# A 31-tap depthwise convolution dealt out anew between ScalarE, GpSimd and VectorE, and a mixing layer in another order

## The chip, the cores and the metric

One Trainium2 chip, one of its cores. The number is the device time of one execution in microseconds; smaller is better. The kernel is a single launch that computes two transformer-like blocks in fp32 for 512 positions of width 1024.

## The reference, cut to what matters

The change lies in the mixing layer of the first block. Everything is fp32; `u` is 512 x 1024.

```python
u = modulate(x, sh2, sc2)
proj = u @ w_in                                    # 1024 x 6144
xr, gr, conf_in, gate_a, gate_b = split(proj)      # 1024, 1024, 2048, 1024, 1024 columns

xr = causal_depthwise_conv(xr, rnn_conv_w, rnn_conv_b)     # 4 taps
r, i = sigmoid(xr @ w_r + b_r), sigmoid(xr @ w_i + b_i)    # per head, 8 heads of 128
log_a = -8 * softplus(-lam) * r
h = scan(exp(log_a), sqrt(-expm1(2 * log_a)) * (i * xr))   # linear recurrence over positions
ya = (h * gelu(gr)) @ rnn_w_proj

glu = conf_in[..., :1024] * sigmoid(conf_in[..., 1024:])
hb = causal_depthwise_conv(glu, conf_dw_w, conf_dw_b)      # 31 taps
hb = silu(layer_norm(hb, conf_ln_g, conf_ln_b))
yb = hb @ conf_w_proj

merged = sigmoid(gate_a) * ya + sigmoid(gate_b) * yb
x = layer_norm(ALPHA * x + (1 + g2) * (merged @ mix_w_out), ln2_g, ln2_b)
```

## The kernel before

Activations lie with features on the partitions: a tensor of 512 x 1024 is eight tiles f = 0..7 of 128 x 512. A product with a weight matrix is made in chunks. A chunk is 256 output columns: its 1 MB of weights comes by DMA from SyncE's queue into one of two slots of `WRAW`; ScalarE copies it rounded to fp32r into `WHI` (`hi`, L555), VectorE makes the rest `WLO` (`lo`, L975), and TensorE runs 48 matmuls of 128x128 by 128x512 (two tiles, eight k, three products of high and low parts; `gemm_chunk`, L1758). ScalarE may overwrite a slot when the chunk two before is done, TensorE starts a chunk when `WLO` is made (`w_lo`) and when its pair of PSUM banks was read out (`free0` or `free1`). `PHASES` (L60) gives the order of all chunks; `CB` and `UB` are the numbers at which a phase begins. Every engine works through its own list in the written order; a wait holds all that is behind it on that engine.

The phases of the mixing layer, in the order of TensorE before the change: `conf` (8 chunks, the input of the long convolution), `xr` (4), `gr` (4), then 16 single matmuls `ri` for r and i (L1960 to L1967), `gb` (4), `ga` (4), `ya` (4), `yb` (4), `mix` (4).

- ScalarE: after each `hi` it reads out PSUM. `conf`: sigmoid into `STG` (L684). `xr`: copy into `XR`. `gr`: gelu into `G` (L697), which lies in the 16 KB of scratch per partition at `T0`. `ri`: sigmoid, tanh, exp (L703 to L712). `gate` (L714): sigmoid of `gb` and `ga` into `STG`, then a store to DRAM; `STG` shares its place with `IT`, the scratch of the recurrence, so a gate first waits until VectorE's 16 steps with it are done (`bt_step` 16). Later it loads the gates back (`SGA`, `SGB`).
- The 31 taps of a tile are 31 multiply-adds over 512 positions. VectorE does tiles 3 to 7 (`conv_taps`, L1232), one instruction a tap, with the running sum in PSUM bank 7; it inserts a written number of taps after its `lo` steps. GpSimd does tiles 0 to 2 (L452 to L466), two instructions a tap: a TENSOR_SCALAR into `TAP`, and a TENSOR_TENSOR that adds it to `HB`.
- VectorE besides: the 4-tap convolution (L1270, L1273), products of the recurrence (L1282 to L1293), then for each tile the scan and the product with gelu (`scan`, L1300), the split of `h * gelu` into `YH` and `YL`.
- The layer norm of the convolution: GpSimd sums six tiles (`ln_sum`, L420), TensorE makes a shift of it (`ln_shift(1)`, ahead of `ya`), VectorE subtracts it, ScalarE squares, GpSimd sums the squares, TensorE makes the statistics (`ln_stats(1)`, after `ya`), VectorE normalizes, ScalarE applies silu, and both split the result into `YH` and `YL` for `yb`.

Of the kernel before, what the change touches and what calls it, by code (L numbers as in the profile page):

```python
# [38 lines left out]
POOL_CONV = 3  # L39
# [20 lines left out]
PHASES = [("ffn1", 22, 11), ("down1", 16, 4), ("conf", 8, 4), ("xr", 4, 2), ("gr", 4, 2),  # L60
          ("gb", 4, 2), ("ga", 4, 2), ("ya", 4, 2), ("yb", 4, 2), ("mix", 4, 2),
# [35 lines left out]
def build_program(nc, I, out):  # L97
    ctx = ExitStack()
    with ctx:
        BASE = 16512  # L100

        def at(name, kb, shape, dt=F32):
# [20 lines left out]
        TAP = at("conv_tap", H0 + 85, [P, L])  # L123
# [5 lines left out]
        STG = at("stage4k", H0 + 81, [P, 2, L])  # L129
# [19 lines left out]
        CONF_T = (at("conf_x_sum", 80, [P, L]), at("conf_squares_sum", 82, [P, L]), at("conf_squares", 84, [P, 2, L]))  # L149
        ln_tiles = lambda c: CONF_T if c == 1 else LN_T  # L150

# [108 lines left out]
                 "yb_sum mg_hi mg_lo lam_step conv31 conv31p s5_load s5_pow_load s5_expand s5_t "  # L260
# [21 lines left out]
        def _(sp):  # L282
# [113 lines left out]
        def _(pool):  # L396
# [54 lines left out]

            for f in range(POOL_CONV):  # L452
                pool.wait_ge(s["free1"], UB["conf"] + f // 2 + 1)
                if f == 0:
                    pool.wait_ge(s["pads_ready"], 1)
                for k in range(CONV_C):
                    src = GLU[:, f, k + 2:k + 2 + L]
                    w = col("conf_dw_w_a", 8 * k + f)
                    n = (2 * CONV_C - 1) * f + 2 * k
                    if k == 0:  # L460
                        nc.gpsimd.tensor_scalar(HB[:, f], src, w, col("conf_dw_b", f), ALU.mult, ALU.add).then_inc(s["conv31p"], 1)
                        continue
# [89 lines left out]
        def _(act):  # L552
# [127 lines left out]
            with act.Fori(0, 4) as i:  # L680
# [6 lines left out]
            act.wait_ge(s["pads_ready"], 2)  # L687
            with act.Fori(0, 2) as i:
                for j in range(2):
                    hi_step("xr", i, 2, j)  # L690
                    act.wait_ge(s["mm"], CB["xr"] + 2 * i + j + 1)
                    A(XR[:, bass.ds(4 * i + 2 * j, 2), 8:8 + L], PS[:, 2 * j:2 * j + 2], ACT.Copy).then_inc(free[j], 1)
            with act.Fori(0, 2) as i:
                for j in range(2):
                    hi_step("gr", i, 2, j)
                    act.wait_ge(s["mm"], CB["gr"] + 2 * i + j + 1)
                    A(G[:, bass.ds(4 * i + 2 * j, 2)], PS[:, 2 * j:2 * j + 2], ACT.Gelu_apprx_tanh).then_inc(free[j], 1)  # L697

            for f in range(KT):
# [13 lines left out]

            def gate(ph, dram, i, j):  # L714
                hi_step(ph, i, 2, j)
                n = (4 if ph == "ga" else 0) + 2 * i + j
                act.wait_ge(s["mm"], CB[ph] + 2 * i + j + 1)
                act.wait_ge(s["bt_step"], 16)
                if n:
                    act.wait_ge(s["sgb_store"], 16 * n)  # L720
                A(STG[:], PS[:, 2 * j:2 * j + 2], ACT.Sigmoid).then_inc(free[j], 1)
                act.wait_ge(free[j], UB[ph] + i + 1)
                act.dma_start(dram[:, 4 * i + 2 * j:4 * i + 2 * j + 2, :], STG[:]).then_inc(s["sgb_store"], 16)
            gate("gb", sgb_dram, 0, 0)
            gate("gb", sgb_dram, 0, 1)
# [29 lines left out]
            act.wait_ge(s["xn_ready"], 16)
# [216 lines left out]
        def _(dve):  # L972
# [38 lines left out]
            def ln_normalize(c, src, each, rooting=None):  # L1011
# [13 lines left out]
                dve.wait_ge(s["ln_step"], ln_step(V.reciprocal(RSTD[:], RT[:])))  # L1025

                def scaled(f):
# [3 lines left out]
                    V.tensor_tensor(src[:, f], src[:, f], RSTD[:], ALU.mult).then_inc(s["xn_ready"], 1)  # L1031
# [197 lines left out]
            taps = [(f, k) for f in range(POOL_CONV, KT) for k in range(CONV_C)]  # L1229
# [19 lines left out]
            for i in range(4):  # L1249
# [5 lines left out]
                if i >= 2:  # L1255
                    conv_taps((16, 15)[i - 2])
# [18 lines left out]
            for i in range(2):  # L1275
                for j in range(2):
                    lo_step("gr", i, 2, j)
                    conv_taps((8, 8, 8, 7)[2 * i + j])
# [4 lines left out]
            lo_step("gb", 0, 2, 0)  # L1283
# [11 lines left out]
            lo_step("gb", 0, 2, 1)  # L1295
# [918 lines left out]
```

## Time and profile before

| | us |
|---|---|
| median of 3 runs | 2374.69 |
| the 3 runs | 2377.97, 2372.64, 2374.69 |
| the profiled execution, its own time | 2371.09 |
| its span (first to last instruction) | 2369.1 |
| TensorE busy in the span | 1953.8 (82%) |
| VectorE | 1205.8 (51%) |
| ScalarE | 743.1 (31%) |
| GpSimd | 488.9 (21%) |

The page cuts the span into 40 slices of 59 us; a digit is the busy share of an engine in tenths. TensorE's row is 3999999799978085979999998869996677496877: slices 13 and 15 (0 and 5 where the neighbours have 8 and 9) lie from 770 to 948 us, in the mixing layer. Matmuls overlap in the pipeline, so a busy share is read for where it falls, not for its height.

### The profile page before, as it was taken

The numbers are of one execution on the slowest core, as the hardware profiler recorded it, in microseconds if no ns is written. First come the engines' busy times: TensorE is split into PE (matmuls) and PEld (weight loads), VectorE is DVE, ScalarE is ACT, GpSimd is POOL, SyncE is SP. The second block draws the span as 40 slices with busy tenths as digits, with TensorE's granted clock in tenths as the row PEclk, the third lists the DMA queues.
The fourth block names the chain that finished last, engine by engine and source line by source line (L and its number), as shares of the span: only waits on it lengthen the run. The fifth ranks groups of instructions, "written<-read, shape, count | busy, mean of one in ns | idle before, by whom it ended". The sixth has DMA issues, their size and how long they took to land.

```text
span 2369.1 us, 23466 instructions
## 1 busy us (share of the span) xinstructions
PE 1953.8 (82%) x8848; PEld 1566.9 (66%) x8848; DVE 1205.8 (51%) x1463; ACT 743.1 (31%) x723; POOL 488.9 (21%) x386
## 2 busy tenths in 40 slices
PE   3999999799978085979999998869996677496877
PEld 2788878588757064758888877768873357474645
DVE  4555555639958476463323346633286764144223
ACT  2433322442453013244333335412341211122323
POOL 0311111279999910010000020010000030100000
PEclk8999999899989597989999999979997785698989
DMA  7455554223313211213333234452321070422200
GB/s 254 154 183 178 175 160 148 84 89 107 107 54 124 71 53 67 90 39 107 95 100 97 87 104 134 145 107 81 107 87 64 9 118 29 107 89 89 71 1 36
DMA packets 201885, 236.71 MB, mean 100 GB/s; under 512 B 5627, under 2 KB 184603, under 8 KB 200923
## 3 DMA queue, kind: packets, MB, share of 16 engines
q1 hardware_dynamic: 185067, 171.27, 22.9%
q0 software_dynamic: 14736, 54.04, 8.7%
q10 hardware_dynamic: 2016, 10.49, 1.2%
q8 instruction: 44, 0.72, 0.1%
q14 instruction: 22, 0.18, 0.0%
HBM read 220.58 MB, written 15.20 MB: 100 GB/s over the span
## 4 chain that ended last, share of the span: by engine, by line
PE 36%; DVE 8%; issue 4%; ACT 4%; DMA 4%; POOL 1%; DVEq 0%; ACTq 0%; SPq 0%; POOLq 0%
PE ps L1769 12%; PE ps L1937 9%; PE ps L1821 4%; PE ps L1787 2%; DMA w_raw<-in_s_glu_w 1%; PE ps L2121 1%; PE ps L2127 1%; DVE ret_root L1629 1%; ACT w_hi L559 1%; PE ps L2143 1%; PE ps L1877 1%; PE ps L2045 1%; DMA s_in<-u_scratch 1%; PE ps L2166 1%; DVE w_lo L978 1%
## 5 line engine op out<-in xcount | busy, mean ns | idle before, releaser
L978 DVE TENSOR_TENSOR w_lo<-w_raw,w_hi 128x2048 fp32r<-128x2048 f32 x160 | 375.3, 2345 | 774.3 <-ACT w_hi L559 757.5
L559 ACT ACTIVATE w_hi<-w_raw 128x2048 fp32r<-128x2048 f32 x158 | 302.4, 1914 | 977.5 <-PE ps L1769 547.6
L1769 PE MATMUL ps<-u_hi,w_hi 128*128 128x512 f32 x960 | 383.7, 400 | 72.7 <-DVE u_lo L1692 31.3
L1769 PE MATMUL ps<-u_lo,w_hi 128*128 128x512 f32 x960 | 378.5, 394 | 0.0
L1769 PE MATMUL ps<-u_hi,w_lo 128*128 128x512 f32 x960 | 378.2, 394 | 0.0
L1769 PEld LDWEIGHTS ps<-u_hi,w_hi 128*128 128x128 f32 x960 | 184.0, 192 | 117.8 <-issue 54.8
L1937 PE MATMUL ps<-u_hi,w_hi 128*128 128x512 f32 x656 | 256.9, 392 | 0.3 <-ACT silu_gate L637 0.3
L1937 PE MATMUL ps<-u_lo,w_hi 128*128 128x512 f32 x656 | 255.8, 390 | 0.0
L1937 PE MATMUL ps<-u_hi,w_lo 128*128 128x512 f32 x656 | 255.8, 390 | 0.0
L1769 PEld LDWEIGHTS ps<-u_lo,w_hi 128*128 128x128 f32 x960 | 183.7, 191 | 39.1 <-issue 1.3
L1769 PEld LDWEIGHTS ps<-u_hi,w_lo 128*128 128x128 f32 x960 | 183.1, 191 | 39.0
L464 POOL TENSOR_SCALAR conv_tap<-glu,param_cols 128x512 f32<-128x512 f32 x90 | 187.6, 2085 | 8.8
L1821 PE MATMUL ps<-hid_hi,w_hi 128*128 128x512 f32 x352 | 140.6, 400 | 0.6 <-DVE hid_lo L1148 0.6
L1937 PEld LDWEIGHTS ps<-u_hi,w_hi 128*128 128x128 f32 x656 | 123.5, 188 | 26.0 <-ACT silu_gate L637 0.7
L1937 PEld LDWEIGHTS ps<-u_hi,w_lo 128*128 128x128 f32 x656 | 123.6, 188 | 25.8
L1937 PEld LDWEIGHTS ps<-u_lo,w_hi 128*128 128x128 f32 x656 | 123.6, 188 | 25.4
L1821 PE MATMUL ps<-hid_hi,w_lo 128*128 128x512 f32 x352 | 137.7, 391 | 0.0
L1821 PE MATMUL ps<-hid_lo,w_hi 128*128 128x512 f32 x352 | 137.6, 391 | 0.0
L466 POOL TENSOR_TENSOR conv_out<-conv_out,conv_tap 128x512 f32<-128x512 f32 x90 | 126.9, 1409 | 7.5
L1244 DVE SCALAR_TENSOR_TENSOR ps<-glu,param_cols,ps 128x512 f32<-128x512 f32 x145 | 109.5, 755 | 4.7
L408 POOL DMA_DIRECT2D ada_raw<-in_ada_w x56 | 40.1, 717 | 347.2 <-DVE ada_acc L1082 295.7
L1082 DVE SCALAR_TENSOR_TENSOR ada_acc<-ada_raw,silu_c,ada_acc 128x512 f32<-128x512 f32 x98 | 74.2, 757 | 8.1 <-DMA ada_raw<-in_ada_w 5.5
(423 smaller groups left out, 2800.2 us busy)
## 6 DMA issues: line engine op xcount, KB each, us to landing
w_raw<-in_w_in SPq DMA_DIRECT2D x44, 1024.0 KB, 5.2
ada_raw<-in_ada_w POOLq DMA_DIRECT2D x56, 512.0 KB, 5.0
w_raw<-in_ffn_w_gate SPq DMA_DIRECT2D x22, 1024.0 KB, 5.3
w_raw<-in_ffn_w_up SPq DMA_DIRECT2D x22, 1024.0 KB, 5.3
w_raw<-in_ffn_w_down SPq DMA_DIRECT2D x32, 704.0 KB, 4.6
ada_first<-in_ada_w SPq DMA_DIRECT2D x8, 1024.0 KB, 11.3
w_raw<-in_w_out SPq DMA_DIRECT2D x8, 1024.0 KB, 5.0
w_raw<-in_rnn_w_proj SPq DMA_DIRECT2D x4, 1024.0 KB, 5.6
```

What stands on the lines that cost most here:

```text
L408: pool.dma_start(ADRAW[:, q % 2], wk8(I["ada_w"])[:, 2 * q:2 * q + 2, bass.ds(2 * D + 512 * i, 512)]).then_inc(ada_load[q % 2], 16)
L464: nc.gpsimd.tensor_scalar(TAP[:], src, w, None, ALU.mult).then_inc(s["conv31p"], 1)
L466: nc.gpsimd.tensor_tensor(HB[:, f], HB[:, f], TAP[:], ALU.add).then_inc(s["conv31p"], 1)
L559: A(WHI[:, slot], WRAW[:, slot], ACT.Copy).then_inc(s["w_hi"], 1)
L978: V.tensor_tensor(WLO[:, slot], WRAW[:, slot], WHI[:, slot].bitcast(F32), ALU.subtract).then_inc(s["w_lo"], 1)
L1082: ins = V.scalar_tensor_tensor(out=acc, in0=ADRAW[:, q % 2, kk], scalar=SC[:, k:k + 1], in1=acc, op0=ALU.mult, op1=ALU.add)
L1244: ins = V.scalar_tensor_tensor(out=dst, in0=src, scalar=w, in1=HACC, op0=ALU.mult, op1=ALU.add)
L1629: V.reciprocal(RRT[:], RRT[:]).then_inc(s["rn"], 1)
L1769: ins = M(PS[:, 2 * j + t, 0:n], w[:, j, at_:at_ + P], a[:, k, 0:n], start=(q == 0), stop=(q == 3 * KT - 1))
L1787: ins = M(PS[:, 2 * j + t], w[:, j, at_:at_ + P], a[:, k], start=(k == 0 and q == 0), stop=(k == KT - 1 and q == 2))
L1821: ins = M(PS[:, 2 * (j // 2)], w[:, j % 2, P * kk:P * kk + P], a[:, k], start=(k == 0 and q == 0), stop=(k == FT - 1 and q == 2))
L1937: ins = M(PS[:, 2 * j + t], w[:, j, at_:at_ + P], a[:, k], start=(q == 0), stop=(q == 3 * KT - 1))
```

## The change

`POOL_CONV` is now tiles 0, 2, 4, 6 and `DVE_CONV` tiles 1, 3, 5, 7. For the first four ScalarE makes the product of each tap (Copy with a scale, or Identity with scale and bias for the first, straight into `HB`) into a ring of four tiles `TAP`, in portions of six after its own steps, and GpSimd only adds. The order of the phases becomes `conf`, `xr`, `gb`, `ri`, `ga`, `gr`, `ya`, `yb`; SyncE's stream follows. `STG` has a place of its own, `G` holds one pair of tiles instead of eight, and `SGA`, `SGB` and the split of the norm's result (`CHI`, `CLO`) lie elsewhere. On TensorE the norm's shift and statistics stand between the chunks of `ya`. ScalarE's loops over `conf`, `xr` and `gr` are written out.

```diff
+POOL_CONV = (0, 2, 4, 6)
+DVE_CONV = (1, 3, 5, 7)
 # PHASES: ... conf, xr, gb, ga, gr, ya ...

 # GpSimd
+            for i, f in enumerate(POOL_CONV):
+                for k in range(1, CONV_C):
+                    m = (CONV_C - 1) * i + k - 1
+                    pool.wait_ge(s["conv_tap"], CONV_C * i + k + 1)
+                    if m:
+                        pool.wait_ge(s["conv31p"], m)
+                    nc.gpsimd.tensor_tensor(HB[:, f], HB[:, f], TAP[:, m % 4], ALU.add).then_inc(s["conv31p"], 1)

 # ScalarE
+            def conv_products(n):
+                for f, k in products[made[0]:made[0] + n]:
...
+                        m = (CONV_C - 1) * i + k - 1
+                        if m >= 4:
+                            act.wait_ge(s["conv31p"], m - 3)
+                        ins = A(TAP[:, m % 4], src, ACT.Copy, scale=w)
...
+            for i in range(4):
                 hi_step("conf", i, 2, 0)
...
                 A(STG[:], PS[:, 0:2], ACT.Sigmoid).then_inc(s["free0"], 1)
+                if i:
+                    conv_products(6)
                 hi_step("conf", i, 2, 1)
+                if i:
+                    conv_products(6)
 # xr, gb: hi_step, PSUM read out (gb also stored), conv_products(6), four times each; then ri as before
-                act.wait_ge(s["bt_step"], 16)
+            gate("ga", sga_dram, 0)
             for f in range(KT):
                 act.wait_ge(s["bt_step"], 2 * f + 2)
                 A(TB[:, f], TB[:, f], ACT.Sqrt).then_inc(s["rnn_sqrt"], 1)
+            for n in range(1, 4):
+                gate("ga", sga_dram, n)
+                conv_products(6)
+            for n in range(4):
+                act.wait_ge(s["mm"], CB["gr"] + n + 1)
+                if n:
+                    act.wait_ge(s["yf_ready"], n)
+                A(G[:], PS[:, 2 * (n % 2):2 * (n % 2) + 2], ACT.Gelu_apprx_tanh).then_inc(free[n % 2], 1)
+                hi_step("gr", n // 2, 2, n % 2)
+                conv_products(6)
+                act.wait_ge(s["yf_ready"], n + 1)
+                A(YH[:, 2 * n:2 * n + 2], XC[:, 2 * n:2 * n + 2], ACT.Copy).then_inc(s["yh_ready"], 2)
             act.wait_ge(s["sgb_store"], 128)
+            act.wait_ge(s["mm"], CB["ya"])
             act.dma_start(SGA[:], sga_dram).then_inc(s["sg_load"], 16)
             hi_step("ya", 0, 2, 0)
             hi_step("ya", 0, 2, 1)
+            ln_squares(1, HB, 0, 8)
             hi_step("ya", 1, 2, 0)
             ln_root(1)
             for f in range(KT + 1):
...
+                if f == 3:
+                    hi_step("ya", 1, 2, 1)

 # VectorE: conv_taps(18) in conf i = 1..3 (before: 16, 15 in i = 2, 3); 8 after each gb step;
 # none after the products of the recurrence; all eight scans behind the two steps of ga i = 0; 6 after each step of ga i = 1
+            for n in range(4):
+                dve.wait_ge(s["scan_done"], 2 * KT)
+                dve.wait_ge(free[n % 2], UB["gr"] + n // 2 + 1)
+                xp = XC[:, 2 * n:2 * n + 2]
+                V.tensor_tensor(xp, xp, G[:], ALU.mult).then_inc(s["yf_ready"], 1)
+                lo_step("gr", n // 2, 2, n % 2)
+                conv_taps(3)
+                dve.wait_ge(s["yh_ready"], 2 * n + 2)
+                V.tensor_tensor(YL[:, 2 * n:2 * n + 2], xp, YH[:, 2 * n:2 * n + 2].bitcast(F32), ALU.subtract).then_inc(s["yl_ready"], 2)
             dve.wait_ge(s["sg_load"], 16)
+            conv_taps(14)
+            lo_step("ya", 0, 2, 0)
+            ya_pair(0)
+            lo_step("ya", 0, 2, 1)
+            ya_pair(1)
+            ln_shift(1, HB, 0, 8)
+            lo_step("ya", 1, 2, 0)
+            ya_pair(2)
+            # ln_normalize; behind its tile 3: ya_pair(3), lo_step("ya", 1, 2, 1)

 # TensorE
             gemm("xr", 2, UH, UL)
+            gemm("gb", 2, UH, UL)
...
             gemm("ga", 2, UH, UL)
+            gemm("gr", 2, UH, UL)
+            gemm_chunk("ya", 0, 0, YH, YL, ready=lambda k: (s["yl_ready"], k + 1))
+            gemm_chunk("ya", 0, 1, YH, YL)
             ln_shift(1)
+            gemm_chunk("ya", 1, 0, YH, YL)
             ln_stats(1, HB, 7)
+            gemm_chunk("ya", 1, 1, YH, YL)
+            gemm_after("yb", 2, CHI, CLO, lambda k: (s["yl_ready"], 8 + k + 1))
```

`lo_step(ph, i, 2, j)` makes the weights of the chunk two further on: that of `gr` with n = 3 makes those of `ya`'s second chunk, that of `ya` (1, 1) those of `yb`'s second.

## Rows read from the trace of the kernel before

**Rows 1.** Who TensorE waited for, 600 to 1010 us: total, times, longest.

```profile
PE ps L1851 <- POOL conf_x_sum L430: 64.9, 1, 64.9
PE ps L1864 <- DVE conv_out L1009: 17.5, 1, 17.5
PE ps L1769 <- ACT stage4k L721: 13.8, 1, 13.8
PE ps L1787 <- DVE y_lo L1337: 10.8, 2, 10.4
...
PE ps L1769 <- DVE ya L1327: 4.1, 1, 4.1
PE ps L1769 <- DVE stage4k L1348: 3.0, 1, 3.0
```

**Rows 2.** Busy time by stretch: PE, PEld, DVE, ACT, POOL, then clock, DMA share, GB/s.

```profile
563.60:639.80 76.20, 76.20 (x338) 63.04 (x337) 75.31 (x68) 25.19 (x18) 72.75 (x40) 1.00 0.31 100
639.80:968.70 328.90, 210.85 (x811) 159.74 (x811) 215.66 (x222) 96.58 (x111) 189.49 (x114) 0.81 0.23 77
```

**Rows 3.** Timeline of ScalarE, weight copies released by a chunk's end: start, duration, idle before.

```profile
639.83 1.91 ACT L559 ACTIVATE w_hi<-w_raw 128x2048 fp32r<-128x2048 f32 x1 [6.62 <-PE ps L1769]
...
708.35 1.92 ACT L559 ACTIVATE w_hi<-w_raw 128x2048 fp32r<-128x2048 f32 x1 [4.06 <-PE ps L1769]
...
968.68 1.92 ACT L559 ACTIVATE w_hi<-w_raw 128x2048 fp32r<-128x2048 f32 x1 [3.04 <-PE ps L1769]
```

**Rows 4.** Timeline of TensorE: last matmul of `ri`; first of the third `gb` chunk.

```profile
657.88 1.12 PE L1967 MATMUL ps<-xr_conv,rglru_w 128*128 128x512 f32 x2
...
694.58 0.79 PE L1769 MATMUL ps<-u_hi,w_hi 128*128 128x512 f32 x1 [13.77 <-ACT stage4k L721]
```

**Rows 5.** The page's costliest groups: GpSimd's two instructions of a tap.

```profile
L464 POOL TENSOR_SCALAR conv_tap<-glu,param_cols 128x512 f32<-128x512 f32 x90 | 187.6, 2085 | 8.8
L466 POOL TENSOR_TENSOR conv_out<-conv_out,conv_tap 128x512 f32<-128x512 f32 x90 | 126.9, 1409 | 7.5
```

**Rows 6.** Timeline of GpSimd: four sums in a row, VectorE idle.

```profile
823.83 5.48 POOL L430 TENSOR_TENSOR conf_x_sum<-conf_x_sum,conv_out 128x512 f32<-128x512 f32 x4
```

**Rows 7.** Timeline of ScalarE: eight activations with a scale per partition.

```profile
660.20 5.01 ACT L709 ACTIVATE rnn_t<-rnn_a,lam_cols 128x512 f32<-128x512 f32 x8
```

**Rows 8.** Timeline of VectorE, 732 to 742 us: a weight rest, then the scans.

```profile
732.05 2.29 DVE L978 TENSOR_TENSOR w_lo<-w_raw,w_hi 128x2048 fp32r<-128x2048 f32 x1 [3.92 <-ACT w_hi L559]
734.26 1.78 DVE L1302 TENSOR_TENSOR rnn_t<-rnn_t,xr_conv 128x512 f32<-128x512 f32 x1
...
739.33 0.68 DVE L1302 TENSOR_TENSOR rnn_t<-rnn_t,xr_conv 128x512 f32<-128x512 f32 x1
740.05 1.51 DVE L1305 TENSOR_TENSOR_SCAN xr_conv<-rnn_a,rnn_t 128x512 f32<-128x512 f32 x1
```

**Rows 9.** Timeline of GpSimd: the addition that falls into these.

```profile
732.50 3.00 POOL L466 TENSOR_TENSOR conv_out<-conv_out,conv_tap 128x512 f32<-128x512 f32 x1
```

**Rows 10.** Timeline of VectorE: one step of the 4-tap convolution and the next weight rest.

```profile
571.03 1.79 DVE L1270 TENSOR_SCALAR xr_conv<-xr_pad,param_cols  x2
572.74 7.00 DVE L1273 SCALAR_TENSOR_TENSOR xr_conv<-xr_pad,param_cols,xr_conv  x6
579.67 3.38 DVE L978 TENSOR_TENSOR w_lo<-w_raw,w_hi 128x2048 fp32r<-128x2048 f32 x1
```

**Rows 11.** The page's groups: VectorE's taps, and a multiply-add all in SBUF elsewhere.

```profile
L1244 DVE SCALAR_TENSOR_TENSOR ps<-glu,param_cols,ps 128x512 f32<-128x512 f32 x145 | 109.5, 755 | 4.7
...
L1082 DVE SCALAR_TENSOR_TENSOR ada_acc<-ada_raw,silu_c,ada_acc 128x512 f32<-128x512 f32 x98 | 74.2, 757 | 8.1 <-DMA ada_raw<-in_ada_w 5.5
```

**Rows 12.** Timeline of VectorE: the norm's first and last steps by tile.

```profile
913.03 1.29 DVE L1031 TENSOR_TENSOR conv_out<-conv_out,rstd 128x512 f32<-128x512 f32 x2
...
934.17 1.29 DVE L1337 TENSOR_TENSOR y_lo<-conv_out,y_hi 128x512 fp32r<-128x512 f32 x2 [1.40 <-ACT y_hi L753]
```

**Rows 13.** The DMA view, issues: the gate's load, KB each, us to landing.

```profile
sig_gate_a<-sga_scratch ACTq DMA_DIRECT2D x1, 2048.0 KB, 8.1
```

More of the change, by code:

```diff
@@ L678, in _ @@
             ln_modulate_hi(0, 0, 8, 0)
-            with act.Fori(0, 4) as i:
+            products = [(f, k) for f in POOL_CONV for k in range(CONV_C)]
+            made = [0]
+            def conv_products(n):
+                for f, k in products[made[0]:made[0] + n]:
+                    src = GLU[:, f, k + 2:k + 2 + L]
+                    w = col("conf_dw_w_a", 8 * k + f)
+                    i = POOL_CONV.index(f)
+                    if k == 0:
+                        act.wait_ge(s["free1"], UB["conf"] + f // 2 + 1)
+                        ins = A(HB[:, f], src, ACT.Identity, scale=w, bias=col("conf_dw_b", f))
+                    else:
+                        m = (CONV_C - 1) * i + k - 1
+                        if m >= 4:
+                            act.wait_ge(s["conv31p"], m - 3)
+                        ins = A(TAP[:, m % 4], src, ACT.Copy, scale=w)
+                    ins.then_inc(s["conv_tap"], 1)
+                    made[0] += 1
+            act.wait_ge(s["pads_ready"], 2)
+            for i in range(4):
                 hi_step("conf", i, 2, 0)
@@ L684, in _, with gate @@
                 A(STG[:], PS[:, 0:2], ACT.Sigmoid).then_inc(s["free0"], 1)
+                if i:
+                    conv_products(6)
                 hi_step("conf", i, 2, 1)
[L687 to L697, printed above, removed]
+                if i:
+                    conv_products(6)
+            for n in range(4):
+                hi_step("xr", n // 2, 2, n % 2)
+                act.wait_ge(s["mm"], CB["xr"] + n + 1)
+                A(XR[:, 2 * n:2 * n + 2, 8:8 + L], PS[:, 2 * (n % 2):2 * (n % 2) + 2], ACT.Copy).then_inc(free[n % 2], 1)
+                conv_products(6)
+            def gate(ph, dram, n):
+                hi_step(ph, n // 2, 2, n % 2)
+                m = (4 if ph == "ga" else 0) + n
+                j = n % 2
+                act.wait_ge(s["mm"], CB[ph] + n + 1)
+                if m:
+                    act.wait_ge(s["sgb_store"], 16 * m)
+                A(STG[:], PS[:, 2 * j:2 * j + 2], ACT.Sigmoid).then_inc(free[j], 1)
+                act.wait_ge(free[j], UB[ph] + n // 2 + 1)
+                act.dma_start(dram[:, 2 * n:2 * n + 2, :], STG[:]).then_inc(s["sgb_store"], 16)
+            for n in range(4):
+                gate("gb", sgb_dram, n)
+                conv_products(6)
             for f in range(KT):
@@ L1227, in _ @@
             ln_normalize(0, X, ln_modulate_lo(0, 0, 8))
-            taps = [(f, k) for f in range(POOL_CONV, KT) for k in range(CONV_C)]
+            taps = [(f, k) for f in DVE_CONV for k in range(CONV_C)]
             done = [0]
@@ L1274, in _ @@
                             ins.then_inc(s["conv4"], 1)
[L1275 to L1278, printed above, removed]
+            for n in range(4):
+                lo_step("gb", n // 2, 2, n % 2)
+                conv_taps(8)
             for f in range(KT):
```

146 lines of the change are left out of this document (51 added, 95 removed).

## The prediction

> **What bounds the kernel now.** I read the slices first: TensorE is busy nearly everywhere except in the mixing layer. There the waits of TensorE name the places [rows 1]. The longest, 64.9 us, is one wait of `ln_shift(1)`, which stands ahead of `ya`, for GpSimd's sum of the convolution; then 17.5 for VectorE's last taps ahead of the statistics, 13.8 for the gate's `STG`, 10.8 for the norm's result, 4.1 and 3.0 for readouts. By stretch [rows 2]: from 563.6 to 639.8 TensorE has no gap at clock 1.00, seven chunks in 76.2 us, 10.88 us a chunk. From 639.8 to 968.7, the ends of `gr` and of `yb` [rows 3], it has 16 chunks (174.1 us), the 16 matmuls of `ri` (to about 658.4, 18.6 us [rows 4]) and the norm's six matmuls, for which I set 5.6 us (an estimate from their busy time). 328.9 - 198.3 = 130.6 us are idle time or slow clock (0.81 on the mean). This is the sum from which the change can take.
>
> GpSimd needs two instructions a tap [rows 5]: 2085 + 1409 ns and the gaps, 3.6 us, times 93 taps, all of 334 us. It began as soon as it could. So before, GpSimd's list is the path from the middle of `conf` to `ya`.
>
> **What goes.** ScalarE makes 124 products and GpSimd 120 additions. A sum of this shape takes GpSimd 5.48 / 4 = 1.37 us, gaps included [rows 6]; 120 of them 164 us. A product costs ScalarE 5.01 / 8 = 0.63 us (an activation with a scale per partition, [rows 7]). A portion of six is thus 3.8 us of ScalarE and 8.2 us of GpSimd, in a chunk of 10.88. The ring of four lets ScalarE finish a portion about 6 us after its start; with the weight copy (1.92) and the PSUM readout (1.0) it is back in 9 us. Behind a portion there wait the next `hi`, and so `lo` and TensorE; 9 < 10.88 covers it, and a portion of 8 us would end the cover. The portions end with the last `gr` chunk (the last has four), so the additions end some 3 us later, the sum of six tiles (5 x 1.37 = 6.9) lies beside `ya`'s first two chunks (21.8), and the 64.9 us go. The 13.8 go with `STG`'s own place, and with them the slow restart (the chunk begun at 694.58 ended at 708.35: 13.8 instead of 10.9, +2.9 [rows 3, 4]). VectorE has 124 taps instead of 155: 31 x 0.79 (755 ns [rows 11] and a gap) = 24 us less, and only 14 are left for after `gr`.
>
> **What comes in its place**, in TensorE's order:
> 1. *VectorE's own work against the additions, `xr` and `gb`.* The taps with their sum in PSUM keep 755 ns whatever GpSimd does. Instructions with two SBUF inputs don't. A step of the 4-tap convolution took 1.79 + 7.00 = 8.65 us from start to next start [rows 10], against 8 x 0.757 = 6.06 by the free multiply-add [rows 11]: 2.6 us more, beside some 2.5 additions of GpSimd, so 1.05 us each. The same at 734.26: 1.78 against 0.68, while the addition begun at 732.50 ran 3.00 (it waited for `w_lo` to end) [rows 8, 9]. They take turns. After the change six additions fall into each step instead of 2.5: 6.06 + 6 x 1.05 + 2.29 for `w_lo` = 14.65 us, against a chunk of 10.88: 3.8 too long, four times 15, less 2 us that VectorE is ahead: 13 us. Lower end 0 (GpSimd waits each time, VectorE never: 8.35 < 10.88); upper end 23 (a full addition of 1.37 each: 16.6 a step). I take 13, what the nearest rows give. The `gb` steps (2.3 + 8 x 0.79 = 8.6) only stop the loss.
>    The Trainium skill, "SBUF — State Buffer", section "SBUF: two separate sides", says that VectorE with two SBUF inputs and GpSimd take turns on one port pair, each for the whole instruction. By that this item would be near its upper end, 23, and the forecast 10 us later. Rows 8 and 9 agree as to the addition; rows 10 don't for GpSimd's one-input product, which lies beside VectorE's work nearly free.
> 2. *`ri`.* ScalarE comes to it behind a portion, and VectorE behind 8 taps instead of 7: +2 us (0 to 4). `ga`'s first two chunks cover tanh, exp and the products; GpSimd is idle there, and the weight rest of the third `ga` chunk, now behind all 16 of VectorE's steps, is ready as it is needed: 0 (0 to 5).
> 3. *Scans.* Now 0.68 + 1.51 us each, without the product with gelu (2.2, [rows 8]), but the last four lie beside two portions: two additions each, 4 x (2.2 + 2 x 1.05) = 17 us and 2.3 for `w_lo`, where TensorE gives about 12.5: +6.8 us ahead of `gr` (0 to 10).
> 4. *`gr` to `ya`.* gelu, product, `YH`, `YL` of the last pair come behind the last `gr` chunk: gelu 1.0, weight copy 1.9, four products 3, `YH` 1.1, `YL` 1.2 and hand-overs, 9 us, of which `ya`'s first six k (18 matmuls, 4.1) hide half: 4.7, and 2.5 for the additions beside it: 7.2 (4 to 10).
> 5. *`ya`.* VectorE waits for the gate's load (8.1 us, [rows 13], now issued after `gr`), then makes 14 taps (11.0), then the rest of weights and the readout for the third chunk: 3.1 late (1 to 6). The statistics wait for GpSimd's sum of squares: 3.5 (2 to 7), instead of 17.5.
> 6. *`yb`.* The normalization takes about 7 us to its first tile and then 22.4 (913.03 to 935.4, [rows 12]), beside `ya`'s last chunk (10.9). But `yb` begins only when its second chunk's weights are made, behind tile 3 (half of the 22.4, 11.2) plus copy, readout and rest (5.4), 0.8 after the statistics in all 24.4 - 10.9 = 13.5: I set 13.4 us of idleness, and 2.9 of slow clock; before, 10.8 and its slow clock. Then 1.5 for a readout. 17.8 together (12 to 26).
>
> Sum: 13 + 2 + 6.8 + 7.2 + 3.1 + 3.5 + 17.8 = 53.4 us in the place of 130.6: 77 us less. What follows `yb` is unchanged. The profiled execution took 2371.1, so 2294; it lies 3.6 below the median of the runs: **2297 us**.
>
> Besides, the page "ScalarE: Activation LUTs" of the Trainium skill, section "What ACT_TABLE_LOAD costs", counts about 1.38 us of drain on top of each load; the loads here stand as 1283 ns, and by the page the one ahead of gelu and the two of the norm would add up to 4 us to the forecast.
>
> **The rivals.**
> - *The port costs nothing* (GpSimd waits, VectorE doesn't). For it: GpSimd's addition at 732.50 did wait; and its additions leave gaps of 2.7 us in a chunk. Against it: rows 10. Items 1, 3 and 2.5 of item 4 go, 22 us, less 2 for a later VectorE in `xr`: 2277.
> - *The ring holds ScalarE.* If the additions come at 2.0 us, as in turns of 0.7 and 1.3, a portion of six needs 12 us > 10.88: 1.1 x 20 portions = 22, and item 1 at its upper end, 10 more: 2329. For it: its mean of 1409 ns and a gap [rows 5] are already over the free 1.37 [rows 6]. Against: VectorE works with two SBUF inputs in only part of the time.
> - *The norm's tail is longer.* Everything up to `ya` as forecast, but the interleaving of copies behind tile 3 and a restart at low clock cost 15 more: 2312.
> - *Slower.* One mechanism: ScalarE is in order, and a product may wait for an addition four back. If the additions take 3.0 us as that of 732.50 throughout, 3.1 with the gap, a portion takes 18.6, each chunk from the second pair of `conf` to `gr` ends 7.7 late, 20 x 7.7 = 154 us, against the 97 that the change brings without items 1 and 3: 2374.7 + 57 = 2432. It decides from a pitch p with 20 x (6p - 10.88) = 97, p = 2.6 us. Against it: in 90 additions the mean was 1.4.
>
> **How the numbers follow.** Forecast 2297: 0.47; port free 2277: 0.26; ring 2329: 0.14; tail 2312: 0.09; slower 2432: 0.04. The range goes from 2268 (port free, and items 4 to 6 at their lower ends) to 2328; it holds the first two, the tail and about half of the ring case. Less than 0.2%, 5 us, can't be told from no change: faster 0.95, same 0.01, slower 0.04, the last rival's chance and a remainder.
>
> **What would show it.** The wait of `ln_shift(1)` gone (under 2 us), the wait on `STG` gone; 120 additions with a mean of 1.5 to 1.9 us; the 4-tap step at 12 to 13 us and waits of TensorE for `w_lo` of 10 to 20 us in `xr`, `gb` and at `gr`'s start, near none if the port is free; ScalarE's weight copies released by the chunk's end and not by GpSimd (the ring rival turns that round); an idle stretch of 10 to 17 us ahead of `yb`. The forecast is wrong if TensorE still waits over 10 us for GpSimd, or if the stretch from the start of `conf` to the end of `yb` is not shorter by 60 to 95 us.

## The result, and the profile after

| | before | after |
|---|---|---|
| median of the runs, us | 2374.03 (4 runs) | 2303.65 (4 runs, 2299.68 to 2307.67) |
| ratio | | 0.9701, 95% interval 0.9679 to 0.9723 |
| profiled execution, us | 2371.1 | 2305.54, span 2303.9 |
| mean granted clock | 0.901 | 0.912 |

The kernel is 70.4 us faster; 77 were forecast, and the time lies in the predicted range.

First the page of the changed kernel, its costliest groups: line, engine, operation, names, count | busy, mean ns | idle before them and who ended it. They answer to [rows 5, 7, 11].

```profile
L463 POOL TENSOR_TENSOR conv_out<-conv_out,conv_tap 128x512 f32<-128x512 f32 x120 | 199.2, 1660 | 141.3 <-ACT conv_tap L693 126.0
...
L693 ACT ACTIVATE conv_tap<-glu,param_cols 128x512 f32<-128x512 f32 x120 | 79.6, 715 | 33.0 <-POOL conv_out L463 30.4
L1268 DVE SCALAR_TENSOR_TENSOR ps<-glu,param_cols,ps 128x512 f32<-128x512 f32 x116 | 87.6, 755 | 6.1 <-DMA sig_gate_a<-sga_scratch 2.4
```

GpSimd's convolution is 199 us of work instead of 315 (187.6 + 126.9 in [rows 5]), and it now has spare time: it waits 126 us for products. An addition takes 1660 ns on the mean, more than the 1409 of [rows 5]. VectorE's taps with the sum in PSUM still take 755 ns.

The waits of TensorE, 480 to 960 us (total, times, longest), answer to [rows 1].

```profile
PE ps L1801 <- DVE w_lo L1001: 16.9, 7, 7.2
PE ps L1819 <- DVE w_lo L1001: 12.8, 1, 12.8
PE ps L1801 <- DVE y_lo L1341: 8.1, 2, 7.5
PE ps L1999 <- ACT rnn_a L733: 5.7, 1, 5.7
PE ps L1801 <- DVE u_lo L1385: 5.1, 1, 5.1
PE ps L1896 <- POOL conf_squares_sum L447: 4.9, 1, 4.9
...
PE ps L1801 <- DVE rnn_i L1380: 1.5, 1, 1.5
```

`ln_shift(1)` no longer waits, nor does any readout into `STG`. In their place stand waits for weight rests of VectorE: seven of at most 7.2 us and the one ahead of `yb` (L1819).

Busy time by stretch, from the end of `xr`'s first chunk to the end of `gb` (seven chunks, as in [rows 2]) and on to the end of `yb`; columns as in [rows 2].

```profile
565.32:654.31 88.99, 80.37 (x337) 64.95 (x336) 87.20 (x73) 46.89 (x57) 64.09 (x41) 0.96 0.33 106
654.31:899.01 244.70, 204.60 (x811) 156.78 (x810) 170.98 (x157) 126.19 (x152) 96.51 (x58) 0.92 0.28 97
```

The ends of these stretches are weight copies in ScalarE's timeline, released by a chunk's end as in [rows 3]; between them the end of `ya`'s first chunk.

```profile
654.31 1.91 ACT L556 ACTIVATE w_hi<-w_raw 128x2048 fp32r<-128x2048 f32 x1 [3.29 <-PE ps L1801]
...
793.53 1.92 ACT L556 ACTIVATE w_hi<-w_raw 128x2048 fp32r<-128x2048 f32 x1 [12.93 <-PE ps L1801]
...
899.01 1.92 ACT L556 ACTIVATE w_hi<-w_raw 128x2048 fp32r<-128x2048 f32 x1 [3.04 <-PE ps L1801]
```

The first stretch took 76.2 and is now 12.8 us longer; from the end of `conf`'s first chunk to its start another 1.0 was lost, nearly all of it in `xr`'s first chunk. The second took 328.9 and is 84.2 shorter. Together 70.4, as much as the medians differ by; that the two agree so closely is chance, since the profiled executions differ by 65.6. From `yb`'s end to the end of the span the kernel before took 1400.6 us and this one 1405.1, in unchanged phases; with the same code there, e6 below took 1408.6 and e7 1401.5. Of the second stretch 198.3 us are the same matmuls as before, so 46.4 us of idleness and slow clock are left in it; the forecast had 40.4 there.

Where VectorE loses time in `xr`: one step of its 4-tap convolution between two weight rests, as in [rows 10].

```profile
587.14 3.36 DVE L1001 TENSOR_TENSOR w_lo<-w_raw,w_hi 128x2048 fp32r<-128x2048 f32 x1
590.42 2.92 DVE L1294 TENSOR_SCALAR xr_conv<-xr_pad,param_cols  x2
593.27 9.25 DVE L1297 SCALAR_TENSOR_TENSOR xr_conv<-xr_pad,param_cols,xr_conv  x6
602.44 2.28 DVE L1001 TENSOR_TENSOR w_lo<-w_raw,w_hi 128x2048 fp32r<-128x2048 f32 x1
604.64 0.99 DVE L1294 TENSOR_SCALAR xr_conv<-xr_pad,param_cols  x2
```

From rest to rest 15.3 us, in a chunk of 10.88: the step is 12.0 instead of 8.65. The last two multiply-adds of this step by themselves, asked for in narrow windows of the same timeline; an addition of GpSimd begins at 599.75 and lasts 1.56, and behind 601.30 GpSimd is idle.

```profile
600.08 1.78 DVE L1297 SCALAR_TENSOR_TENSOR xr_conv<-xr_pad,param_cols,xr_conv  x1
601.77 0.74 DVE L1297 SCALAR_TENSOR_TENSOR xr_conv<-xr_pad,param_cols,xr_conv  x1
```

So an addition costs a multiply-add with two SBUF inputs 1.04 us. The TENSOR_SCALARs, with one SBUF input and an SBUF output, pay as much: two take 2.92 us beside the additions and 0.99 with GpSimd idle (604.64). Further on in the same timeline the scans: the early ones with GpSimd idle, the late ones beside its additions.

```profile
702.97 0.67 DVE L1320 TENSOR_TENSOR rnn_t<-rnn_t,xr_conv 128x512 f32<-128x512 f32 x1
703.67 1.23 DVE L1322 TENSOR_TENSOR_SCAN xr_conv<-rnn_a,rnn_t 128x512 f32<-128x512 f32 x1
704.82 3.32 DVE L1001 TENSOR_TENSOR w_lo<-w_raw,w_hi 128x2048 fp32r<-128x2048 f32 x1
708.06 1.78 DVE L1320 TENSOR_TENSOR rnn_t<-rnn_t,xr_conv 128x512 f32<-128x512 f32 x1
709.87 2.21 DVE L1322 TENSOR_TENSOR_SCAN xr_conv<-rnn_a,rnn_t 128x512 f32<-128x512 f32 x1
...
723.56 3.29 DVE L1001 TENSOR_TENSOR w_lo<-w_raw,w_hi 128x2048 fp32r<-128x2048 f32 x1
```

GpSimd's timeline has one row for the late ones.

```profile
704.21 26.64 POOL L463 TENSOR_TENSOR conv_out<-conv_out,conv_tap 128x512 f32<-128x512 f32 x13 [37.22 <-ACT conv_tap L693]
```

Beside the additions a product takes 1.7 to 1.8 us instead of 0.67 and a scan 2.2 instead of 1.22; the additions themselves come every 26.64 / 13 = 2.05 us instead of 1.37 [rows 6]. The two engines take turns. The rest at 723.56 is the one that `gr` waits for. In TensorE's timeline this wait, and the one ahead of `yb`, look so:

```profile
719.42 0.39 PE L1801 MATMUL ps<-u_hi,w_lo 128*128 128x512 f32 x1
726.99 0.79 PE L1801 MATMUL ps<-u_hi,w_hi 128*128 128x512 f32 x1 [7.18 <-DVE w_lo L1001]
727.57 0.63 PE L1801 MATMUL ps<-u_lo,w_hi 128*128 128x512 f32 x1
728.00 0.63 PE L1801 MATMUL ps<-u_hi,w_lo 128*128 128x512 f32 x1
...
837.53 0.39 PE L1801 MATMUL ps<-y_hi,w_lo 128*128 128x512 f32 x1
850.70 0.77 PE L1819 MATMUL ps<-conf_hi,w_hi 128*128 128x512 f32 x1 [12.78 <-DVE w_lo L1001]
```

Before the wait a matmul starts every 0.23 us, after it every 0.43: the clock stands at its lower level (1.2 GHz) and rises again a few us later (granted clock 0.87 on the mean from 727 to 739, 1.00 from 745 to 770). The waits of 4.9 to 12.8 us ahead of `gr`, `ya`, the statistics and `yb` are each paid twice, by 1.1 to 3.3 us. In `xr` and `gb` too the chunks behind waits of 3.6 and 2.3 us, at 590.56 and 630.55, ran at a mean clock of 0.88 and 0.87 and took 1.7 and 1.9 us more than their wait; those behind 1.7 and 1.1 us ran at 1.00.

### The profile page after: what moved, and what is told of

Read it like the earlier page. It is cut to its first block, busy times and chain, and to the rows that moved or that the text cites. A ratio compares the mean times of both kernels' runs of the same rounds, so it can differ in the third digit from the quotient of the medians.

```text
span 2303.9 us, 23558 instructions
## 1 busy us (share of the span) xinstructions
PE 1955.2 (85%) x8848; PEld 1567.7 (68%) x8848; DVE 1189.0 (52%) x1424; ACT 808.4 (35%) x832; POOL 368.2 (16%) x323
## 4 chain that ended last, share of the span: by engine, by line
PE 38%; DVE 8%; issue 4%; DMA 4%; ACT 4%; POOL 1%; DVEq 0%; ACTq 0%; SPq 0%; POOLq 0%
PE ps L1801 12%; PE ps L1969 9%; PE ps L1853 4%; PE ps L1819 2%; DMA w_raw<-in_s_glu_w 1%; PE ps L2156 1%; PE ps L2162 1%; DVE ret_root L1661 1%; PE ps L2178 1%; ACT w_hi L556 1%; PE ps L1909 1%; DMA s_in<-u_scratch 1%; PE ps L2080 1%; PE ps L2201 1%; DVE s_state L1624 1%
## 5 line engine op out<-in xcount | busy, mean ns | idle before, releaser
L463 POOL TENSOR_TENSOR conv_out<-conv_out,conv_tap 128x512 f32<-128x512 f32 x120 | 199.2, 1660 | 141.3 <-ACT conv_tap L693 126.0
L693 ACT ACTIVATE conv_tap<-glu,param_cols 128x512 f32<-128x512 f32 x120 | 79.6, 715 | 33.0 <-POOL conv_out L463 30.4
L1268 DVE SCALAR_TENSOR_TENSOR ps<-glu,param_cols,ps 128x512 f32<-128x512 f32 x116 | 87.6, 755 | 6.1 <-DMA sig_gate_a<-sga_scratch 2.4
```

Source lines behind the costliest of these rows:

```text
L463: nc.gpsimd.tensor_tensor(HB[:, f], HB[:, f], TAP[:, m % 4], ALU.add).then_inc(s["conv31p"], 1)
L693: ins = A(TAP[:, m % 4], src, ACT.Copy, scale=w)
L1268: ins = V.scalar_tensor_tensor(out=dst, in0=src, scalar=w, in1=HACC, op0=ALU.mult, op1=ALU.add)
```

## The experiments

All are edits of the changed kernel; times are medians, and ratios are to the kernel before in the same set of runs. "Net" is the shift of a chunk's end against the changed kernel, less the shift at `conf`'s first matmul. The ratios are known to some 0.0022 to either side, so two kernels that are less than 7 us apart can't be told from equal by their times. The profiles have a scatter of their own: e2, e3, e4 and e6 have the changed kernel's code up to the end of `gb`, and yet end it 3.8 to 4.3 us earlier net; 2.5 us of that go again in `ri`. e3, which has this code up to `ya`, ends the first `gr` chunk 1.1 us earlier net, and that much of the shifts of e4 and e6 is not their edit's doing. The theory: GpSimd's additions and VectorE's instructions with two SBUF inputs take turns, which costs TensorE `w_lo` waits; the norm's place in `ya` and ScalarE's products bring the gain. The rivals: it costs nothing; ScalarE's ring of four, or its own load, delays the weight copies; the order of the phases alone brings the gain.

**e1_conv4_in_psum**: the 4-tap convolution's running sum lies in PSUM.

```diff
-                            dst = XC[:, bass.ds(f, 1)]
+                            acc = PS[:, 5 + t]
...
-                                ins = V.scalar_tensor_tensor(out=dst, in0=src, scalar=w, in1=dst, ...)
+                                ins = V.scalar_tensor_tensor(out=XC[:, f] if k == CONV_R - 1 else acc, in0=src, scalar=w, in1=acc, ...)
```

> The changed kernel, with the running sum of the 4-tap convolution in PSUM banks 5 and 6, so that none of its 32 instructions reads two SBUF tensors (only the last of each tile writes SBUF); VectorE's loop over xr is written out. Port theory (GpSimd's additions and VectorE's instructions with two SBUF inputs take turns): a step falls from 12.2 to 6.5 us, TensorE's waits for w_lo in xr and gb (9.7 us) and the slow clock behind them go, the fourth gb chunk ends at 642 to 644 instead of 654.3, the time is 10 to 12 us lower, about 2293. Rival (VectorE's list ahead of these chunks is simply too long by the taps moved there, wherever the operands lie): the step stays near 12 us, the time within 2 us of 2303.7.

Measured: 2291.67 us (2286.56 to 2294.56), ratio 0.9644 (0.9621 to 0.9666): 12.0 us less than the changed kernel. VectorE's timeline, the step that answers to the one at 590.42:

```profile
582.24 1.52 DVE L1296 TENSOR_SCALAR ps<-xr_pad,param_cols 128x512 f32<-128x512 f32 x2
583.66 2.72 DVE L1298 SCALAR_TENSOR_TENSOR ps<-xr_pad,param_cols,ps 128x512 f32<-128x512 f32 x4
586.30 1.40 DVE L1298 SCALAR_TENSOR_TENSOR xr_conv<-xr_pad,param_cols,ps 128x512 f32<-128x512 f32 x2
```

The step takes 5.5 us instead of 12.0 with the same arithmetic and the same additions beside it. From `conf` to `gb`, TensorE's waits for `w_lo` shrink from 9.7 to 1.1 us (the 7.2 ahead of `gr` stay), and from `xr`'s second chunk on the chunks end every 10.88 us; the fourth `gb` chunk ends at 640.63 (654.31; net 12.9 earlier). This settles item 1: the turns made 12.9 us of its 13.8. The ring of four and ScalarE's load were the same in this kernel, so by themselves they delay no chunk there.

**e2_norm_around_ya**: TensorE's norm matmuls moved out of `ya`, all else as in the changed kernel.

```diff
             gemm("gr", 2, UH, UL)
+            ln_shift(1)
             gemm_chunk("ya", 0, 0, YH, YL, ready=lambda k: (s["yl_ready"], k + 1))
...
-            ln_shift(1)
             gemm_chunk("ya", 1, 0, YH, YL)
-            ln_stats(1, HB, 7)
             gemm_chunk("ya", 1, 1, YH, YL)
+            ln_stats(1, HB, 7)
```

> The changed kernel with one part undone: on TensorE the norm's shift stands ahead of the four ya chunks and the statistics behind them, as before the change. Theory (the interleaving hides one chunk under the normalization, and the shift ahead of ya waits for the last additions and the sum of six tiles): ya starts 15 us later at 790, but ends its first chunk only 7 us later since it no longer starts early; the normalization is exposed by one chunk less; yb ends some 12 us later: 2314 to 2318. Rival (yb waits for its second chunk's weights anyway, so the place of the statistics costs nothing): at most 3 us, 2303 to 2307.

Measured: 2317.2 us, ratio 0.9755 (0.9735 to 0.9776): 13.5 us more. The waits of TensorE:

```profile
PE ps L1819 <- DVE w_lo L1001: 23.7, 1, 23.7
PE ps L1883 <- POOL conf_x_sum L435: 21.7, 1, 21.7
```

The time is as expected (2314 to 2318). GpSimd's sum of the tiles is 21.7 us behind `gr` even now: the additions end at 786.8 here and at 787.2 in the changed kernel, some 15 us behind `gr` where the prediction had some 3. In the changed kernel the sum still lies beside `ya`'s first two chunks, which end at 804.4. TensorE's wait ahead of `yb` grows from 12.8 to 23.7, as the statistics now have no chunk beside the normalization. So 13.5 us of the gain hang on the place of shift and statistics together; the two were not run apart.

**e3_yb_weights_tile1**: the weights of `yb`'s second chunk made behind tile 1 of the norm, not 3.

```diff
-                if f == 3:
+                if f == 1:
                     hi_step("ya", 1, 2, 1)
...
-                if f == 3:
+                if f == 1:
                     ya_pair(3)
                     lo_step("ya", 1, 2, 1)
```

> The changed kernel with the copy of yb's second weights, the last ya readout and the weight rest behind the norm's tile 1 instead of tile 3. Theory (TensorE's 12.8 us ahead of yb are the wait for these weights): yb starts at 844 instead of 850.7, and its first pair ends when the last normalized tile allows, near 867 instead of 874.5: 6 to 8 us less, about 2297. Rival (the pace of the normalized tiles bounds yb in any case): TensorE's wait only changes its name, 0 to 2 us less.

Measured: 2302.12 us, ratio 0.9707 (0.9677 to 0.9736): 1.5 us less, not to be told from none; by the time alone the rival holds. TensorE's wait:

```profile
PE ps L1819 <- DVE w_lo L1001: 9.5, 1, 9.5
```

ScalarE's timeline at the place:

```profile
836.65 1.91 ACT L556 ACTIVATE w_hi<-w_raw 128x2048 fp32r<-128x2048 f32 x1 [1.97 <-PE ps L1801]
838.47 0.61 ACT L776 ACTIVATE conf_hi<-conv_out 128x512 fp32r<-128x512 f32 x1
```

The wait shrank by 3.3 us and not by the 6 to 8 expected. The copy (1.91) is released only by the end of the chunk before, and now stands ahead of the first `conf_hi` instead of behind the third, so the tiles that `yb` begins with come later by it. `yb` ended 2.8 us earlier, counted from the end of `ya`'s first chunk, and its readouts waited for the second gate's load, which ScalarE issues only behind the norm's last tile. The weights' place is a part of item 6; the distance from the statistics to the first tiles is the rest.

**e4_gr_weights_in_scans**: the weight rest for `gr`'s first chunk behind scan 5 instead of 7.

```diff
             for f in range(4, KT):
                 scan(f)
-            for j in range(2):
-                lo_step("ga", 1, 2, j)
-                conv_taps(6)
+                if f == 5:
+                    lo_step("ga", 1, 2, 0)
+            conv_taps(6)
+            lo_step("ga", 1, 2, 1)
+            conv_taps(6)
```

> The changed kernel with the weight rest of the first gr chunk behind the sixth scan instead of the eighth. Theory (the 7.2 us ahead of gr are the last scans, stretched by the additions, in VectorE's list; behind them TensorE restarts at low clock, 1.8 us): both go, the first gr chunk ends at 731 instead of 739.7, 8 to 9 us less, about 2295. Rival (the scans then end 3 us later and the product with gelu waits for them; or ScalarE's portions hold the next copy): the wait moves to ahead of the third gr chunk or of ya, 0 to 4 us less.

Measured: 2299.51 us, ratio 0.9687 (0.9664 to 0.9709): 4.1 us less, which the times can't tell from none; in the profile `yb` ends 4.4 us earlier net, 1.1 of them as in e3. TensorE's waits:

```profile
PE ps L1803 <- DVE w_lo L1001: 10.2, 6, 3.9
PE ps L1803 <- DVE y_lo L1343: 7.9, 2, 7.5
```

The first `gr` chunk ended 8.5 us earlier net; the second chunk's rest, still behind all scans, then cost 3.9. The scans were the bound, and moving one rest out of them only passes half of the wait on.

**e5_pool_makes_products**: ScalarE makes no products. GpSimd makes products and sums of three tiles, VectorE five tiles; phases, norm and buffers as changed.

```diff
-POOL_CONV = (0, 2, 4, 6)
-DVE_CONV = (1, 3, 5, 7)
+POOL_CONV = (0, 2, 4)
+DVE_CONV = (1, 3, 5, 6, 7)
...
+                    nc.gpsimd.tensor_scalar(TAP[:, 0], src, w, None, ALU.mult).then_inc(s["conv31p"], 1)
...
-            products = [(f, k) for f in POOL_CONV for k in range(CONV_C)]
+            products = []
...
-            conv_taps(14)
+            conv_taps(45)
```

> The changed kernel with one part undone: ScalarE makes no products; GpSimd makes products and sums of three tiles (0, 2, 4) as before the change, VectorE takes the five others, its 31 more taps in the portion behind gr. The new order of the phases and the norm's place stay. Theory (the long wait was GpSimd's list alone, and the order of the phases only removes the wait on the gates' scratch): GpSimd ends near 822 and its sum near 829 as before the change, VectorE's portion of 45 taps near 822; the shift behind ya's second chunk waits 25 to 30 us, so the time is 2325 to 2340, and of the 70 us some 40 to 45 stay with the new order and the norm within ya, 25 to 30 with ScalarE's products. Rival (ScalarE's products carry most of it): over 2350.

Measured: 2331.53 us, ratio 0.9818 (0.9801 to 0.9836): 27.9 us more than with ScalarE's products, and 43 less than the kernel before in the same set. TensorE's longest wait, expected at 25 to 30 us:

```profile
PE ps L1891 <- POOL conf_x_sum L435: 39.0, 1, 39.0
```

Busy time in the four chunks of `gb`, columns as before:

```profile
597.37:641.01 43.64, 43.64 (x193) 35.94 (x192) 42.96 (x41) 11.31 (x8) 41.64 (x24) 1.00 0.45 153
```

So some 43 of the 70 us come from the new order, `STG`'s own place and the norm's place in `ya`, and 28 net from ScalarE's products with the tiles dealt out four and four; these pay for the turns and save more by taking the convolution's end away. The order was not run by itself: of the 43, e2 gives 13.5 to the norm's place, if that is worth the same here, and some 30 are left for order and `STG`. TensorE has no gap in these four chunks, nor in the last three of `xr` ahead of them, with GpSimd busy in 41.6 of 43.6 us. VectorE's 4-tap step takes 8.6 to 8.8 us in `xr`, as in [rows 10]: two or three additions stand in it instead of six or seven, and products of GpSimd between them.

**e6_scan_from_psum**: the product ahead of a scan is written to PSUM, and the scan reads it there.

```diff
-                V.tensor_tensor(TB[:, f], TB[:, f], XC[:, f], ALU.mult)...
+                V.tensor_tensor(PS[:, 4 + f % 2], TB[:, f], XC[:, f], ALU.mult)...
...
-                V.tensor_tensor_scan(XC[:, f], RA[:, f], TB[:, f], 0.0, ...)
+                V.tensor_tensor_scan(XC[:, f], RA[:, f], PS[:, 4 + f % 2], 0.0, ...)
```

> The changed kernel, with the product ahead of each scan written to PSUM (banks 4 and 5 in turn), so that the scan reads one SBUF tensor instead of two. Port theory: of the four late scans each loses one of its two turns (the scan falls from 2.2 to 1.2 us, the product stays at 1.7), the group from 15.5 to 11.6 us, TensorE's 7.2 us ahead of gr fall to about 3, the time is 4 to 6 us lower, about 2299. Rival (the scan is slow by its own dependence, not by the port): no change of the scan's 2.2 us, time within 1 us.

Measured: 2296.18 us, ratio 0.966 (0.9638 to 0.9682): 7.5 us less. The late scans in VectorE's timeline:

```profile
704.93 1.78 DVE L1322 TENSOR_TENSOR ps<-rnn_t,xr_conv 128x512 f32<-128x512 f32 x1
706.75 1.22 DVE L1324 TENSOR_TENSOR_SCAN xr_conv<-rnn_a,ps 128x512 f32<-128x512 f32 x1
707.89 0.67 DVE L1322 TENSOR_TENSOR ps<-rnn_t,xr_conv 128x512 f32<-128x512 f32 x1
...
713.43 2.27 DVE L1001 TENSOR_TENSOR w_lo<-w_raw,w_hi 128x2048 fp32r<-128x2048 f32 x1
```

GpSimd's timeline beside them, in one row, and two of these additions in narrow windows:

```profile
701.56 19.59 POOL L463 TENSOR_TENSOR conv_out<-conv_out,conv_tap 128x512 f32<-128x512 f32 x10 [38.28 <-ACT conv_tap L693]
...
706.30 1.57 POOL L463 TENSOR_TENSOR conv_out<-conv_out,conv_tap 128x512 f32<-128x512 f32 x1
708.01 1.70 POOL L463 TENSOR_TENSOR conv_out<-conv_out,conv_tap 128x512 f32<-128x512 f32 x1
```

Four pairs take 8.5 us instead of 15.5. More than expected was gained, as not only the scans but also the products behind the first ran at 0.67, though they still have two SBUF inputs. The rows show why: an addition ran beside each scan (706.30 to 707.87 beside the one at 706.75), so each product began as an addition had just ended (707.89), and the next addition, begun at 708.01, was the one that waited: 1.70 instead of 1.29 us. `yb` ended 7.4 us earlier net, 1.1 of them as in e3 (4 to 6 expected).

**e7_combined**: e1, e3, e4 and e6 together. Besides, `gr`'s second rest goes ahead of the taps; the last gelu pair is split into `YH` and `YL` before ScalarE's next copy and products and VectorE's next rest and taps; the second gate's load is issued at tile 1 of the norm; and 17 taps stand ahead of the wait for the first gate.

```diff
-                hi_step("gr", n // 2, 2, n % 2)
-                conv_products(6)
+                if n < 3:
+                    hi_step("gr", n // 2, 2, n % 2)
+                    conv_products(6)
                 act.wait_ge(s["yf_ready"], n + 1)
                 A(YH[:, 2 * n:2 * n + 2], XC[:, 2 * n:2 * n + 2], ACT.Copy)...
+            hi_step("gr", 1, 2, 1)
+            conv_products(6)
...
+                if f == 1:
                     hi_step("ya", 1, 2, 1)
+                    act.wait_ge(s["mm"], CB["yb"])
+                    act.dma_start(SGB[:], sgb_dram)...
...
-            dve.wait_ge(s["sg_load"], 16)
...
-            conv_taps(14)
+            conv_taps(17)
+            dve.wait_ge(s["sg_load"], 16)
```

> The edits that gained, together: 4-tap sums and scan inputs in PSUM; the rests of the first two gr chunks' weights behind scans 6 and 8 and ahead of the taps; the last gelu pair split ahead of its copy, products and taps; 17 taps ahead of the wait for the gate's load; yb's second weights behind the norm's tile 1 with the second gate's load issued there. By the port theory and the waits read: 10 to 12 us from xr and gb, 7 to 9 ahead of gr, 4 to 6 ahead of ya, 2 to 4 ahead of yb: 2273 to 2281. Rival (each removed wait of VectorE turns up at the next one, since its list is full from conf to ya): no more than the 12 us of the first, about 2290.

Measured: **2279.3 us** (2272.43 to 2281.96, 5 runs), as expected, ratio 0.9594 (0.9577 to 0.9611): 24.4 us, 1.1%, below the changed kernel, and the fastest of all. TensorE's waits:

```profile
PE ps L1829 <- DVE w_lo L1004: 9.5, 1, 9.5
...
PE ps L1811 <- DVE y_lo L1349: 6.2, 2, 3.2
```

In the profiled execution, the fastest of the five (2272.43), `yb` ends 28.2 us earlier net. The sum of the single runs is 25.1 (12.0 + 7.5 + 4.1 + 1.5), of which the last two can't be told from none, so nothing shows that the extra edits brought more than e3 and e4 had left undone. The split of the last pair halves the longest `y_lo` wait (7.5 to 3.2); it was not run alone.

## Why the prediction was right, step by step

- **Direction and size.** The 64.9 and 13.8 us waits went, as said, and 60.2 us of other idleness took the place of 130.6, where the sum had 53.4. The mechanisms named were there; the 6.8 us too few come from sizes, and in item 1 two errors cancelled.
- **Item 1, `xr` and `gb`: 13 forecast, 13.8 measured, in part by luck.** The price of 1.05 us an addition, read from the 4-tap step and from 1.78 against 0.68 [rows 8, 10], is right (1.78 - 0.74 = 1.04). The count under it isn't. Without GpSimd a TENSOR_SCALAR took 0.54 us and a multiply-add 0.74, started every 0.46 and 0.66, so the bare step is 4.9 us and not 6.06; and in the first two steps not six but seven instructions waited for an addition. 4.9 + 7 x 1.02 = 12.0, where the sum had 12.4. The four steps took 12.1, 12.0, 9.1 and 10.1, since GpSimd ran out of products in the last two (5.5 and 2.0 us of idleness), and the rests between them up to 3.38. So TensorE waited only 9.2 us, in five pieces; the other 4.6 are the restarts behind them, 3.6 of them slow clock, which the sum did not have. In e2, e3, e4 and e6, with the same code, the item was 9.9 and `ri` 5.3 to 5.5; the two together were 16.6 here and 15.2 to 15.4 there, against 15 forecast.
  The bare step also shows that GpSimd's one-input products are not nearly free, as the prediction read from rows 10. Of the 8.65 us there, 4.9 are bare, 2.1 go to two additions, and 1.7 stand beside products. VectorE's and GpSimd's timelines of the kernel before, in narrow windows:

```profile
577.91 1.18 DVE L1273 SCALAR_TENSOR_TENSOR xr_conv<-xr_pad,param_cols,xr_conv  x1
577.53 1.89 POOL L464 TENSOR_SCALAR conv_tap<-glu,param_cols 128x512 f32<-128x512 f32 x1
```

  A multiply-add beside a product took 1.18 us instead of 0.74, and the product 1.89 instead of 1.57; in e5 it is 1.17 and 1.89. So a product costs VectorE 0.44 us, an addition 1.04.
  The Trainium skill, "SBUF — State Buffer", section "SBUF: two separate sides", has VectorE with two SBUF inputs and GpSimd lock each other out for a whole instruction. Each VectorE instruction does wait at most for one addition, in line with it; but 0.67 became 1.7 and not 2.0 (0.67 + 1.37), and the multiply-add at 577.91 began and ended while a product of GpSimd was recorded as running (577.53 to 579.42).
- **Item 2, `ri`: 2 forecast, 2.8 measured** (TensorE took 21.6 us from its first matmul to `ga` instead of 18.8); no wait at `ga`'s third chunk.
- **Item 3, scans: 6.8 forecast, 9.0 measured**: a wait of 7.2 and 1.8 of slow clock behind it. The wait was sized well, the clock left out.
- **Item 4, `gr` to `ya`: 7.2 forecast, 10.3 measured**: two waits for `y_lo` (8.1) and 2.2 of slow clock.
- **Item 5: `ya`'s third chunk 3.1 forecast, nothing measured**: VectorE stood idle for the gate's load for 2.4 us (the group of L1268 above) and not for its whole 8.1 [rows 13], since it was itself late from item 4, and the third chunk's rest was in time. **Statistics 3.5 forecast, 6.0 measured**: wait 4.9, slow clock 1.1.
- **Item 6, `yb`: 17.8 forecast, 17.6 measured**: a wait of 12.8 (13.4), slow clock 3.3 (2.9), readout 1.5 (1.5). The four chunks last 899.01 - 850.70 = 48.3 us instead of 43.5.
- **The mis-sized term** is thus the slow clock behind waits: 1.8 + 2.2 + 1.1 = 5.1 us in items 3, 4 and 5, and 3.6 in item 1. It was counted for `yb` and for the old `STG` wait only. In item 1 it made up for waits that were shorter than forecast; of the 6.8 us the items account for some 6.
- **The table loads.** The 4 us that the prediction counts besides its sum, for a drain on top of each load, don't show: in the changed kernel the load at 690.57 follows 0.02 us behind the weight copy and lasts 1.28 us, and the next activation starts at 691.86; so it is with the two loads of the norm (821.95, 829.47), as far as ScalarE had work ready.
- **The rivals.** The port is not free: e1 gains 12.0 by taking its cost away. The ring rival needed additions every 2.0 us throughout; they came every 1.7 in `xr`, and every 2.0 only beside the scans and in `gr`. Though ScalarE waited 30.4 us for GpSimd in 32 pieces of at most 2.6 us, its weight copies were still released by chunk ends in `xr` and `gb`, and e1, with the same ring, has no gap there from `xr`'s second chunk on. In `ga` one copy (709.95) stood right behind a product that had waited 2.6 us for GpSimd, so there the ring did hold ScalarE; no wait of TensorE is put down to it. The tail came as forecast. The slower case needed a pitch of 2.6 us; the worst stretch had 2.05 on the mean, and single additions of 3.15 stood only beside weight rests.

What stays open: how the port chooses. The runs bound its price for a VectorE instruction (0 to 1.1 us an addition, by where its operands lie and whether an addition is running as it starts) and don't show its rule.

## What to carry to other kernels

When work moves to GpSimd or between engines, list for each stretch which instructions of VectorE have two SBUF inputs, or are a TENSOR_SCALAR from SBUF to SBUF; beside GpSimd's additions each was some 1 us longer here, and the remedy is cheap: keep a running sum, or one operand of a scan, in PSUM. Place long vector work beside TensorE's chunks by splitting the serial part (here the norm) between them; that was worth 13.5 us (e2), beside 28 net for ScalarE's products (e5). For each new wait of TensorE add its slow restart as a term, also where the wait is short: it cost 1.7 and 1.9 us behind waits of 3.6 and 2.3. And compare a profile's shift with that of another run that has the same code up to there: here identical code moved a mark by 4 us.

## What the runs showed of the hardware

- Beside GpSimd additions of 128x512, VectorE's two-input product went from 0.67 to 1.7 or 1.8 us, its multiply-add from 0.74 to 1.78, its scan from 1.22 to 2.2, a weight rest of 128x2048 from 2.28 to 3.36, and a TENSOR_SCALAR from SBUF to SBUF, with one SBUF input, from 0.54 to 1.50. With one operand in PSUM a multiply-add stayed at 0.7 to 0.76 and a scan at 1.22.
- Beside GpSimd's one-input products a two-input multiply-add went from 0.74 to 1.18.
- In e6 the additions ran beside the scans; the products behind the first came just as an addition had ended and took 0.67 us, and the additions begun beside them took 1.70 us instead of 1.29.
- A wait of 7.2 us was enough for TensorE to restart at half rate (0.43 us a matmul instead of 0.23); so was one of 3.6 us, and behind one of 4.9 us the granted clock was 0.56 (821.0 to 826.4).
